# Second attention's softplus: magnitude on ScalarE instead of a clamp on VectorE, and the diagonal mask moved into the scores

## The reference, cut to what matters

```python
z = jnp.einsum('bqhd,bkhd->bhqk', qb, kf) * (B_DH ** -0.5)
valid = k_pos[None, :] < qpb[:, None]
log_keep = jnp.where(valid, jax.nn.log_sigmoid(-z), 0.0)
after = lax.cumsum(log_keep, axis=3, reverse=True) - log_keep
a = jnp.where(valid, jnp.exp(jax.nn.log_sigmoid(z) + after), 0.0)
out = jnp.einsum('bhqk,bkhd->bqhd', a, vf)
```

## Time and profile before

| | us |
|---|---|
| median of 3 runs (2124.23 to 2124.6) | 2124.3 |
| the profiled execution: its own time | 2126.75 |
| the profiled execution: span | 2125.0 |
| busy in the span: PE / PEld | 1911.1 / 1637.2 |
| busy in the span: DVE / ACT / POOL | 1255.2 / 1005.7 / 323.0 |
| mean granted clock of PE, as a share of full | 0.957 |

### The profile page before, as it was taken

The page is one execution under the profiler, slowest core; times in us unless marked ns, Lnnn a source line. Parts: engine busy times, 40 slices in busy tenths (PEclk is TensorE's granted clock), DMA queues, the critical chain, the costliest instruction groups (busy, mean ns, idle before and its releaser), DMA issues. The chain is left out here.

```text
span 2125.0 us, 35549 instructions
## 1 busy us (share of the span) xinstructions
PE 1911.1 (90%) x11420; PEld 1637.2 (77%) x11420; DVE 1255.2 (59%) x2661; ACT 1005.7 (47%) x2361; POOL 323.0 (15%) x541
## 2 busy tenths in 40 slices
PE   3999989999899889996799999999999999689995
PEld 2877878878778689986777777777777778479995
DVE  4456555564554622454286868686868686844455
ACT  5455454554554622454254555454545454522345
POOL 0111111111111000264010101110101011100341
PEclk7999999999999889998999999999999999979999
DMA  4121111211111232211111111010111111133213
GB/s 130 51 63 49 48 45 56 60 35 45 55 56 49 92 104 84 70 64 57 36 46 36 45 35 55 26 55 25 55 35 45 44 37 46 72 101 96 63 47 122
DMA packets 161891, 124.22 MB, mean 58 GB/s; under 512 B 11136, under 2 KB 152768, under 8 KB 161792
## 3 DMA queue, kind: packets, MB, share of 16 engines
q1 hardware_dynamic: 161792, 123.08, 18.8%
HBM read 89.53 MB, written 33.52 MB: 58 GB/s over the span
## 5 line engine op out<-in xcount | busy, mean ns | idle before, releaser
L105 PE MATMUL lb_pj<-lb_w_high,h_high 128*128 128x384 f32 (+1 forms) x576 | 209.1, 363 | 19.4 <-DVE lb_w_low L1265 10.3
L105 PE MATMUL la_pj<-la_w_high,h_high 128*128 128x384 f32 (+1 forms) x576 | 208.0, 361 | 6.9 <-DVE la_w_low L569 6.9
L1132 ACT ACTIVATE lb_m<-lb_m 128x512 f32<-128x512 f32 (+4 forms) x200 | 98.8, 521 | 236.5 <-DVE lb_m L1286 235.3
L105 PE MATMUL lb_pj<-lb_w_high,h_low 128*128 128x384 f32 (+1 forms) x576 | 200.8, 349 | 0.0
L105 PE MATMUL lb_pj<-lb_w_low,h_high 128*128 128x384 f32 (+1 forms) x576 | 200.0, 347 | 0.0
L105 PE MATMUL la_pj<-la_w_low,h_high 128*128 128x384 f32 (+1 forms) x576 | 195.9, 340 | 0.0
L105 PE MATMUL la_pj<-la_w_high,h_low 128*128 128x384 f32 (+1 forms) x576 | 195.0, 339 | 0.0
L1457 POOL TENSOR_TENSOR lb_o<-lb_o,lb_keep 128x512 f32<-128x512 f32 (+3 forms) x80 | 77.3, 967 | 649.0 <-ACT lb_keep L1156 649.0
L1299 DVE TENSOR_TENSOR lb_s<-lb_sc,lb_m 128x512 f32<-128x512 f32 (+4 forms) x200 | 110.1, 550 | 61.3 <-ACT lb_m L1137 61.2
L418 ACT ACTIVATE la_p<-la_sc,la_nm 128x128 f32<-128x128 f32 (+5 forms) x144 | 106.1, 739 | 57.8 <-DVE la_nm L608 56.0
L105 PEld LDWEIGHTS lb_pj<-lb_w_high,h_high 128*128 128x128 f32 (+1 forms) x576 | 108.4, 188 | 29.4 <-issue 11.7
(11 more groups left out here) (295 smaller groups left out, 5197.4 us busy)
## 6 DMA issues: line engine op xcount, KB each, us to landing
stage<-in_a_w_in SPq DMA_DIRECT2D x60, 192.0 KB, 3.1
stage<-in_b_w_in SPq DMA_DIRECT2D x60, 192.0 KB, 2.9
stage<-in_ple_w_gate SPq DMA_DIRECT2D x22, 512.0 KB, 3.6
h_low<-o_t SPq DMA_DIRECT2D x14, 528.0 KB, 6.5
mix_b_xs<-x_mid SPq DMA_DIRECT2D x8, 528.0 KB
norm_a_xt<-in_x SPq DMA_DIRECT2D x8, 512.0 KB, 3.6
stage<-in_a_w_in SPq DMA_DIRECT2D x16, 256.0 KB, 5.2
out_ak<-la_tok SPq DMA_DIRECT2D x8, 512.0 KB, 3.3
```

The source lines that it names most:

```text
L105: last = pe.matmul(out, x, y, start=start and n == 0, stop=stop and n == 2, **kw)
L1132: act.activation(x, x, ACT.Exp).then_inc(S["exp"], 1)
```

## The change

`clamp` is taken out of DVE's list. ACT gets a new step `size` in its place: m = |z|, read from PSUM, both units of a pair ahead of their `exp`. `exp` then takes exp(-m), `log` is as before, and `softplus` is s = max(z, 0) + m in one DVE instruction, by the identity softplus(z) = max(z, 0) + log(1 + exp(-|z|)). The matmul that adds -1e30 to the masked places moves from `after` to the end of `scores`, so that z itself is masked: there |z| is huge, exp(-|z|) is 0 and s becomes 0 without the multiplication by `strict`, which goes. The constant table `strict_sample` goes with it.

```diff
+                def size(s):
+                    slot, x, _, _ = views(s)
+                    act.wait_ge(S["z"], at.next("z"))
+
+                    act.wait_ge(S["soft"], at.nth("soft", s - 1) if s >= 2 else at.before("soft"))
+                    act.activation(x, slot, ACT.Abs).then_inc(S["size"], 1)
+
                 def exp(s):
                     x = views(s)[1]
-                    act.wait_ge(S["clamped"], at.next("clamped"))
-                    act.activation(x, x, ACT.Exp).then_inc(S["exp"], 1)
+                    act.wait_ge(S["size"], at.next("size"))
+                    act.activation(x, x, ACT.Exp, scale=-1.0).then_inc(S["exp"], 1)
...
                 for i in range(NP + 1):
                     if i < NP:
+                        for s in units(i):
+                            size(s)
                         for s in units(i):
                             exp(s)
...
-                def clamp(s):
-                    slot, x, _, _ = views(s)
-                    dve.wait_ge(S["z"], at.next("z"))
-
-                    dve.wait_ge(S["soft"], at.nth("soft", s - 1) if s >= 2 else at.before("soft"))
-                    dve.tensor_scalar(x, slot, SOFT_MAX, None, ALU.min).then_inc(S["clamped"], 1)
-
                 def softplus(s):
...
-                    ins = dve.tensor_tensor(sp, slot, x, ALU.max)
-                    if c < 2 and not span(c, b)[2]:
+                    ins = dve.scalar_tensor_tensor(out=sp, in0=slot, scalar=0.0, in1=x, op0=ALU.max, op1=ALU.add)
+                    if c < 2:
                         ins.then_inc(S["soft"], 1)
-                    elif c < 2:
-                        ins.then_inc(S["dve_link"], 1)
-                        dve.wait_ge(S["dve_link"], at.next("dve_link"))
-                        dve.tensor_tensor(sp[:, 0:P], sp[:, 0:P], masks["strict"][:, :], ALU.mult).then_inc(S["soft"], 1)
                     else:
                         ins.then_inc(S["dve_link"], 1)
                         dve.wait_ge(S["dve_link"], at.next("dve_link"))
                         new = sp[:, :, PB * DEC:]
-                        dve.tensor_tensor(new, new, masks["strict_sample"][:, :, :], ALU.mult).then_inc(S["dve_link"], 1)
-                        dve.wait_ge(S["dve_link"], at.next("dve_link"))
...
                 for i in range(NP + 1):
-                    if i < NP:
-                        for s in units(i):
-                            clamp(s)
                     if i >= 2:
                         add(i - 2)
...
+                masked = dict(start=False, stop=True, skip_group_check=True)
+
                 def scores(i):
...
+                        for hd in range(2):
+                            last = pe.matmul(slot[:, hd, PB * DEC:], unit[:, :], hide[:, 0:DEC], **masked)
                         last.then_inc(S["z"], 1)
...
                             if n == 2:
+                                if span(c, b)[2]:
+                                    last = pe.matmul(views(s)[0][:, 0:P], unit[:, :], hide[:, :], **masked)
                                 last.then_inc(S["z"], 1)
...
                 def after(s):
...
                         for hd in range(2):
-                            pe.matmul(slot[:, hd, PB * DEC:], unit[:, :], hide[:, 0:DEC], **add)
...
                     else:
-                        if span(c, b)[2]:
-                            pe.matmul(slot[:, 0:P], unit[:, :], hide[:, :], **add)
                         pe.wait_ge(S["low"], at.nth("low", split_before(s) + 1))
```

More of the change, by code:

```diff
@@ L950, in span @@
         return q, QC - q, b >= 4 * c
-    diagonal = sum(c < 2 and b >= 4 * c for c, b, _ in UNITS)
     with ExitStack() as ctx:
@@ L974, in stick_layer @@
                      tok_stored=64, g_ready=3, g_normed=3, g_clamped=3, g_exp=3, g_log=3, g_soft=3, g_sig=3, g_done=3,
-                     z=N, clamped=N, exp=N, log=N, soft=N, high=SPLIT, low=SPLIT, after=N, a=N, sums=CARRIED,
-                     keep=CARRIED, scaled=CARRIED, added=NP - 1, sampled=1, pv=NP, dve_link=diagonal + 5, o_ready=3,
+                     z=N, size=N, exp=N, log=N, soft=N, high=SPLIT, low=SPLIT, after=N, a=N, sums=CARRIED,
+                     keep=CARRIED, scaled=CARRIED, added=NP - 1, sampled=1, pv=NP, dve_link=4, o_ready=3,
                      pe_tick=0, fill=1, pads=1)
@@ L1279, in body @@
                 at, ahead = Count(table, r), Count(table, r + 1)
-                def clamp(s):
-                    slot, x, _, _ = views(s)
-                    dve.wait_ge(S["z"], at.next("z"))
-                    dve.wait_ge(S["soft"], at.nth("soft", s - 1) if s >= 2 else at.before("soft"))
-                    dve.tensor_scalar(x, slot, SOFT_MAX, None, ALU.min).then_inc(S["clamped"], 1)
                 def softplus(s):
-                    c, b, _ = UNITS[s]
+                    c = UNITS[s][0]
                     slot, x, sp, _ = views(s)
@@ L2190, in build @@
         masks = {n: top.enter_context(nc.sbuf_tensor(n, s, F32)) for n, s in
-                 (("neg_tri", [P, P]), ("neg_ones", [P, P]), ("strict", [P, P]), ("strict_sample", [P, 2, DEC]))}
+                 (("neg_tri", [P, P]), ("neg_ones", [P, P]), ("strict", [P, P]))}
         h_offset = -(-nc.sbuf_base // 32) * 32
```

## The result

The changed kernel takes 2109.38 us (median of 5 runs, 2102.67 to 2112.42) against 2124.6 (5 runs of the kernel before beside it): 0.9922 of the time, 95% interval 0.9901 to 0.9942. It is faster by 15 us where 50 were forecast, and lies outside the range of 2061 to 2096. The profiled execution took 2109.38 us, its span is 2107.6, its mean granted clock 0.968 (before 2126.75, 2125.0 and 0.957).

A forecast was written before the change was run, and what follows sets the result against it. PE was taken to set the pace of seven groups and DVE's list that of the eighth; starts 25 + 0.8, middles 14 and eighth group 10 sum to 50 us, giving 2074 us, range 2061 to 2096.

The forecast's parts named there:

- so PE's total is unchanged: Mask matmul moved from after to scores: delays z by at most 0.2 us, shortens after by as much.
- The first rival: At the loop's jump ACT stalls 2.8 us like DVE; starts gain 1.1 us each, total 31.4, 2093 us; chance 0.27.
- The count of all instructions: At the loop's jump: by the skill's fetch rule, this count with waits, and the page boundaries, would decide who stalls.
- VectorE's own stall: At six group starts DVE is back from its jump at 1567.6, before softplus at 1568.3, so hidden.
- the 31 that were forecast: PE's idle time in the seven groups: the forecast's terms for it add up to 31 us.
- Group starts: Six starts gain 2.7 us of waiting and 1.5 of clock each, 25 us; two without a jump 0.4 each.
- the 9 us: Clock stays up behind six starts, 1.5 us each; rival that it falls all the same: 41 gained, 2083, chance 0.14.
- Middles: Middle of seven groups: PE's waits shrink by 2.0 of 2.46 us each, 14 us.
- Eighth group: Pairs of the eighth group: DVE sets the pace; cycle falls from 8.6 to 6.4 us, 10 us in all.
- The prices of Abs and of the mask multiplications: On a pair's chain: two Abs take 1.14 us; dropped mask multiplications, 0.29 us each, save 0.3 per unit.
- The two table loads: On ACT: two loads in the whole span; rival that Abs needs its own table: about 2146 us, chance 0.02.
- The rival that Abs is no earlier than the clamp: ACT not free earlier than the clamp was: waiting pairs get a 0.42 us longer chain, +7, 2131; chance 0.07.

The follow-up runs named there:

- both masks last: The changed kernel with both heads' third scores matmuls issued first in a diagonal pair, then both mask matmuls; 2087.72 us, 0.9811 of the kernel before.
- the parted pass: The changed kernel with both mask matmuls together between the first and the second head's third scores matmul; 2100.19 us, 0.9866 of the kernel before.
- both lists short: Both masks last, with ScalarE's list shortened (four lb_m buffers, softplus in place, implied waits dropped) and VectorE's by implied waits; 2077.89 us, 0.9779 of the kernel before.
- ScalarE's alone: Both masks last, with only ScalarE's list shortened (four lb_m buffers, softplus in place, implied waits dropped); 2087.7 us, 0.9813 of the kernel before.
- the filler between the heads: Both masks last, with half a token tile's projection issued between the two heads' after in pair 1 of each group; 2078.89 us, 0.9762 of the kernel before.

## Why the prediction was wrong

**The step that failed: "so PE's total is unchanged".** The mask matmul was priced by a matmul's duration, and its neighbours were not looked at. PE's total rose by 24.3 us in the seven groups, where a higher clock alone should have cut it by 9: a diagonal pair's two mask matmuls cost 0.93 us in the new place and 0.23 in the old. The order of the two mask matmuls accounts for 21.7 us of the 35 that were missing (both masks last against the change, shown). The earlier trace rows held the warning: "x2" and 0.40 us for two matmuls of 512 columns, as long as one takes alone. The Trainium skill, "TensorEngine Tiling (Array Packing)", section "Key Properties", has it that a change of tiling mode, unlike a change of tile, drains TensorE. The trace agrees in that one more change to and fro costs 0.19 us here; that the parted pass costs 0.23 and the parted masks 0.15 more only the runs show.

**The first rival came true as well.** At the jump ScalarE stalls 2.4 to 2.7 us in all six rounds. The second split ends 9.4 us behind ScalarE's branch; before it was 10.9. That is a gain of 1.5 at this start: the rival said 1.1, the forecast 2.7. Shortening both lists gives 9.8 us (2087.7 to 2077.9, shown), ScalarE's alone none. The reason it was held less likely, that other engines jump freely, counted nothing: POOL's and SP's lists have 38 and 68 instructions. The count of all instructions, which the prediction names and didn't make, decides on ScalarE and VectorE: lists of 233 to 259 jump in 0.3 us or less, lists of 283 to 372 take 2.4 to 3.8. On PE it doesn't: its list has some 700 entries for the weight loads alone and jumps in 0.27. The Trainium skill, "Runtime: NRT & Kernel Launch", section "Instruction fetch mechanics", gives fetch pages of 256 instructions, with two in reach. The trace agrees only so far as lists of about one page jump freely on these two engines and longer ones stall, with more instruction packets. Just where the limit lies between 259 and 283, and what the alignment does to it, no run here tells.

**The two together.** Both masks last and both lists short give 2077.9 us, 4 from the forecast of 2074. That is nearer than the sum deserves: the short lists also took away VectorE's own stall, which the forecast had left in place and called hidden. With ScalarE's stall alone gone the time stayed at 2087.7: VectorE's jump had grown from 2.8 us to 3.5 and was hidden no longer. And that PE's idle time fell by just the 31 that were forecast was luck: with both masks last it fell by 25.9, and the changed kernel's longer scores covered the rest. The range lacked a rival in which PE itself becomes slower.

**Group starts.** Abs, softplus and the splits cost what was said. The clock stays up behind the sixth start, as forecast, but it still falls once in each of five groups, in four of them behind the sample pair. So the time at the lower level went from 30.6 us to 17 in the seven groups, and as half of it is lost, some 7 of the 9 us came back. With the start covered by the filler between the heads only the idle time came back and the clock fell as often as before, so that the clock follows this idle time is not borne out.

**Middles.** One wait of 0.33 is left of 2.46: 2.1 against 2.0 forecast.

**Eighth group.** 10.1 us against 10; cycles of 5.9 and 6.7 against 6.4. PE's longer scores cost nothing there, since PE has time (85 of 103 us busy).

**The prices of Abs and of the mask multiplications** were right. The two table loads are those of the kernel before. The Trainium skill, "ScalarE: Activation LUTs", section "Table sets: the hidden batching unit", has abs in every table set, and the trace agrees. The rival that Abs is no earlier than the clamp is out, since the waits in the middle went.

**Open.** With both masks last a diagonal pair still pays 0.13 us more for them than in `after` (0.36 against 0.23); an order that costs nothing was not found. The part of the missing 35 us that the order (21.7) and the stalls (9.8) leave, some 4 us, is no more than two totals can differ by and wasn't traced. VectorE's list alone was not shortened, so what each of the two stalls costs by itself stays open. Why the changed kernel's runs spread over 10 us wasn't tried.

## What to carry to other kernels

Before moving a matmul, look at the shapes of its neighbours: where two half-height matmuls run side by side ("x2" in the time of one), a full-height one between them costs the pairing and further changes of shape (0.93 us here for two, and 0.36 behind both). Before moving work to another engine inside a hardware loop, count that engine's whole list, waits included, and compare it with lists that are known to jump freely on the same engine. And when a timeline's idle time falls as forecast but the time doesn't, compare busy times at equal instruction counts, and the clock beside them.

## What the runs showed of the hardware

Two 64-row matmuls of different heads run side by side even when one head's three stand ahead of the other's in the kernel's text (0.90 us a pair either way; four full-height ones take 1.03). A jump back in a loop takes 0.24 us on ScalarE with 239 or 259 instructions in the body and 2.4 to 2.7 with 283 or 284; VectorE's take 0.3 with 244, 3.5 with 289 and 2.8 with 372. And the clock fell to 0.51 (1.2 GHz, the lower of two levels) behind a stretch in which PE was busy for 3.40 of 3.40 us, with 42 matmuls, 32 of them of 32 columns.
